# Expert inputs of a mixture layer gathered as 128 half rows instead of 64 whole rows

## What is computed

```
logits = (xf @ w_router) + b_router
top_val, top_idx = lax.top_k(logits, TOP_K)          # 4 of 32
gates = jax.nn.softmax(top_val, axis=-1)
...                                                    # rows sorted by expert
xs = xf[row_tok]
def expert_block(args):
    xb, e = args
    hu = xb @ w_up[e] + b_up[e]
    x_glu = jnp.minimum(hu[:, :D_FF], SWIGLU_LIMIT)
    x_lin = jnp.clip(hu[:, D_FF:], -SWIGLU_LIMIT, SWIGLU_LIMIT)
    act = x_glu * jax.nn.sigmoid(SWIGLU_ALPHA * x_glu) * (x_lin + 1.0)
    return act @ w_down[e] + b_down[e]
out = segment_sum(ys * row_gate, row_tok)             # 2048 rows back to 512 tokens
```

## Time and profile before

| | |
|---|---|
| median of three executions | 2962.32 us |
| the profiled execution, its own time | 2956.22 us |
| its span | 2954.6 us |
| TensorE busy, share of the span | 94% |
| DMA by SP's queue, share of 16 engines | 53.7% (607.76 MB) |
| DMA by POOL's queue | 4.1% (38.12 MB) |
| mean granted TensorE clock | 0.967 |

### The profile page before, as it was taken

The page is one execution under the profiler, slowest core; times in us unless marked ns, Lnnn a source line. Parts: engine busy times, 40 slices in busy tenths (PEclk is TensorE's granted clock), DMA queues, the critical chain, the costliest instruction groups (busy, mean ns, idle before and its releaser), DMA issues.

```text
span 2954.6 us, 37476 instructions
## 1 busy us (share of the span) xinstructions
PE 2770.8 (94%) x15815; PEld 1366.1 (46%) x15815; DVE 1125.3 (38%) x1420; ACT 477.1 (16%) x936; POOL 242.1 (8%) x369
## 2 busy tenths in 40 slices
PE   7998989897889989898999999999999999999998
PEld 3445866332223323232333475467654334556763
DVE  3855454311111111111124253455436652444544
ACT  1113232000000000000001143000023662200001
POOL 1000011112111011110011500000000210000000
PEclk9988988999999999999999999999999999999999
DMA  9776235999999999999999131213132223321310
GB/s 340 286 257 255 74 115 191 385 345 416 384 394 408 409 404 408 407 413 397 413 407 350 9 127 52 86 57 114 57 80 59 66 50 114 107 86 57 114 57 29
DMA packets 172882, 648.23 MB, mean 219 GB/s; under 512 B 75965, under 2 KB 77573, under 8 KB 140305
## 3 DMA queue, kind: packets, MB, share of 16 engines
q1 hardware_dynamic: 156674, 607.76, 53.7%
q0 software_dynamic: 15984, 38.12, 4.1%
q10 hardware_dynamic: 64, 0.07, 0.0%
HBM read 626.43 MB, written 24.06 MB: 220 GB/s over the span
## 4 chain that ended last, share of the span: by engine, by line
PE 78%; DMA 12%; DVE 5%; ACT 2%; DVEq 1%; issue 1%; SPq 0%; ACTq 0%
PE ps L1867 14%; PE ps L2548 10%; PE ps L2583 10%; DMA slots<-in_w_down_dram 8%; PE ps L1905 8%; PE ps L2886 4%; PE ps L2619 4%; PE ps L2257 3%; PE ps L3142 2%; DMA slots<-in_ada_w_dram 2%; PE ps L1913 2%; PE ps L2513 2%; PE ps L2430 2%; PE ps L2533 2%; PE ps L1259 2%; DMA slots<-in_w_ada_dram 2%
## 5 line engine op out<-in xcount | busy, mean ns | idle before, releaser
L1867 PE MATMUL ps<-slots,hT 128*32 128x512 f32 x5120 | 563.2, 598 | 15.4 <-DMA slots<-in_w_up_dram 14.3
L1867 PEld LDWEIGHTS ps<-slots,hT 128*32 128x32 f32 x5120 | 165.5, 111 | 388.3 <-issue 362.6
L2583 PE MATMUL ps<-slots,work 128*128 128x512 f32 x672 | 289.6, 592 | 2.8 <-DVE work L2661 2.8
L1905 PE MATMUL ps<-slots,work 128*32 128x512 f32 x2112 | 247.8, 613 | 45.8 <-DMA slots<-in_w_down_dram 45.3
L2020 DVE TENSOR_SCALAR stage<-ps 128x512 f32<-128x512 f32 (+1 forms) x47 | 32.2, 686 | 549.0 <-PE ps L1871 548.6
L2583 PEld LDWEIGHTS ps<-slots,work 128*128 128x128 f32 x672 | 127.5, 190 | 162.5 <-issue 157.9
L2548 PE MATMUL ps<-hT,slots 128*128 128x256 f32 x768 | 168.7, 379 | 0.0
L1905 PEld LDWEIGHTS ps<-slots,work 128*32 128x32 f32 x2112 | 69.3, 112 | 194.5 <-issue 189.4
L2886 PE MATMUL ps<-hT,slots 128*128 128x512 f32 x352 | 156.8, 601 | 0.0
L2548 PEld LDWEIGHTS ps<-hT,slots 128*128 128x128 f32 x768 | 145.9, 190 | 22.4 <-issue 2.9
L2758 DVE TENSOR_TENSOR work<-work,ps 128x1024 f32<-128x1024 f32 x60 | 71.6, 1218 | 164.8 <-PE ps L2583 164.6
(11 more groups left out here) (610 smaller groups left out, 3447.7 us busy)
## 6 DMA issues: line engine op xcount, KB each, us to landing
slots<-in_w_up_dram SPq DMA_DIRECT2D x128, 2048.0 KB
slots<-in_w_down_dram SPq DMA_DIRECT2D x64, 2048.0 KB
slots<-in_mlp_w_dram SPq DMA_DIRECT2D x32, 2048.0 KB, 7.9
slots<-in_ada_w_dram SPq DMA_DIRECT2D x40, 1024.0 KB, 4.9
slots<-in_w_ada_dram SPq DMA_DIRECT2D x16, 1024.0 KB, 5.4
slots<-in_w_in_dram SPq DMA_DIRECT2D x5, 2048.0 KB
slots<-in_rnn_w_in_dram SPq DMA_DIRECT2D x24, 384.0 KB, 4.2
slots<-in_w_ada_dram SPq DMA_DIRECT2D x4, 2048.0 KB
```

What stands on the lines that cost most here:

```text
L1867: ins = pe.matmul(to, x[:, k, unit * UNIT:(unit + 1) * UNIT], upw[s][:, k % 2, col:col + CH], start=k == 0, stop=False)
L1905: ins = pe.matmul(to, actT[:, 4 * q + j, 64 * u + 32 * h:64 * u + 32 * h + 32], downw[sl[h]][:, j, half * CH:(half + 1) * CH], start=k == ...
L2583: ins = pe.matmul(ps[:, bank + t], x[:, k, t * P:(t + 1) * P], w[:, k], start=k == 0, stop=k == HK - 1)
```

## The change

Each quad is now gathered by 128 indices, 64 rows times two halves: partition `64 h + r` receives half `h` (2 KB) of row `r`. The index table is built with 128 rows, by issuing each of the 16 matmuls of `route_pe` twice, once for output partitions 0 to 63 and once for 64 to 127 with the same operands, and `xsl` holds 2 x token + h. All gathers have 128 indices, those of quads with one unit too; an empty place gets an index beyond the bound as before. A quad then takes four transposes of 128 x 128 in place of eight of 64 rows (or eight for two quads together), one PSUM bank a quad, and ScalarE's copy puts the two halves of the columns in place. The block loop after the passes keeps its gather of 64 whole rows.

```diff
-    k["pairsf"] = ...((pairs + np.array([0, 1]))...
+    rc[:, 241] = r // (2 * UNIT)
+    k["pairsf"] = ...((pairs * np.array([2, 1]) + np.array([0, 1]))...
...
+        h2_halves = h2_dram.rearrange("t (h n) -> (t h) n", h=2)
...
             for a in range(16):
-                ins = pe.matmul(ps[0:64, 4, 0:2 * NQ], in_row[:, a], marks[:, a]..., start=a == 0, stop=a == 15)
+                for h in range(2):
+                    ins = pe.matmul(ps[64 * h:64 * h + 64, 4, 0:2 * NQ], in_row[:, a], marks[:, a]..., start=a == 0, stop=a == 15)
...
-            v.tensor_scalar(xempty, ps[0:64, 4, NQ:2 * NQ], 0.0, float(T), ALU.is_equal, ALU.mult)
+            v.tensor_scalar(xempty, ps[:, 4, NQ:2 * NQ], 0.0, float(2 * T), ALU.is_equal, ALU.mult)
             v.drain()
-            v.tensor_tensor(xsl[:], ps[0:64, 4, 0:NQ], xempty, ALU.add).then_inc(S("route_step"), 1)
+            v.scalar_tensor_tensor(xsl[:], ps[:, 4, 0:NQ], row_half, xempty, ALU.add, ALU.add).then_inc(S("route_step"), 1)
...
-        xg_rest = work[0:64, 6144:7168]
+        xg_rest = work[:, 6144:6144 + CH]
...
+        def x_halves(i, q):
+            return xg[i % 4][:, q * CH:(q + 1) * CH] if q < 2 else xg_rest
...
             for q, units, at in quads(i):
-                n = units * UNIT
-                to = xg[i % 4][q * 64:q * 64 + n] if q < 2 else xg_rest[0:n]
-                g.indirect_dma_start(to, None, h2_dram, bass.IndirectOffsetOnAxis(ap=xsl[0:n, at:at + 1], axis=0),
-                                     bounds_check=T - 1, oob_is_err=False)...
+                g.indirect_dma_start(x_halves(i, q), None, h2_halves, bass.IndirectOffsetOnAxis(ap=xsl[:, at:at + 1], axis=0),
+                                     bounds_check=2 * T - 1, oob_is_err=False)...
...
-                for tile, r0, n, ks in x_runs(i):
-                    for j in range(KT // ks):
-                        if m >= 2:
-                            pe.wait_ge(S("moe_turned_out"), m - 1)
-                        for k in range(ks):
-                            ins = pe.transpose(ps[:, 6 + m % 2, k * n:(k + 1) * n], tile[0:n, (ks * j + k) * P:(ks * j + k + 1) * P], ident[0:n, 0:n])
+                for q, units, at in quads(i):
+                    if m >= 2:
+                        pe.wait_ge(S("moe_turned_out"), m - 1)
+                    for k in range(KT // 2):
+                        ins = pe.transpose(ps[:, 6 + m % 2, k * P:(k + 1) * P], x_halves(i, q)[:, k * P:(k + 1) * P], ident[:])
...
-                        a.copy(xgT[i % 2][:, ks * j:ks * (j + 1), r0:r0 + n],
-                               ps[:, 6 + m % 2, 0:ks * n].rearrange("p (k n) -> p k n", k=ks)).then_inc(S("moe_turned_out"), 1)
+                    a.copy(xgT[i % 2].rearrange("p (h k) n -> p h k n", h=2)[:, :, :, q * n:(q + 1) * n],
+                           ps[:, 6 + m % 2].rearrange("p (k h n) -> p h k n", h=2, n=n)).then_inc(S("moe_turned_out"), 1)
```

More of the change, by code:

```diff
@@ L104, in constants @@
     rc[:, 240] = (r // UNIT) % 2 - 2
+    rc[:, 241] = r // (2 * UNIT)
     k["route"] = rc
-    k["pairsf"] = np.ascontiguousarray((pairs + np.array([0, 1])).astype(np.float32).reshape(P, 16, 2).transpose(0, 2, 1).reshape(P, 32))
+    k["pairsf"] = np.ascontiguousarray((pairs * np.array([2, 1]) + np.array([0, 1])).astype(np.float32).reshape(P, 16, 2).transpose(0, 2, 1).reshape(P, 32))
     return k
@@ L1376, in build @@
         q_edge, w_of, r_base, r_cap = rconst[:, 0:NQ + 1], rconst[:, 64:128], rconst[:, 128:160], rconst[:, 160:192]
-        half_at = rconst[:, 240:241]
+        half_at, row_half = rconst[:, 240:241], rconst[:, 241:242]
         tok_of, dest_of = rconst[:, 256:272], rconst[:, 272:288]
@@ L1390, in build @@
         again = flatT[0:64, 3840:3968]
-        xempty = flatT[0:64, 3968:3968 + NQ]
+        xempty = flatT[:, 3968:3968 + NQ]
         pairs = R0[:, 1800:1800 + 16 * LCOLS].bitcast(I32)
@@ L1394, in build @@
         tab = sb("tab", [1, E + 2 * MAXO + 1], I32)
-        xsl = sb("xsl", [64, NQ], I32)
+        xsl = sb("xsl", [P, NQ], I32)
         ysl = sb("ysl", [P, NQ], I32)
@@ L1454, in route_pe @@
             for a in range(16):
-                ins = pe.matmul(ps[0:64, 4, 0:2 * NQ], in_row[:, a], marks[:, a].rearrange("p two q -> p (two q)"), start=a == 0, stop=a == 15)
+                for h in range(2):
+                    ins = pe.matmul(ps[64 * h:64 * h + 64, 4, 0:2 * NQ], in_row[:, a], marks[:, a].rearrange("p two q -> p (two q)"), start=a == 0, stop=a == 15)
             ins.then_inc(S("route_product"), 1)
@@ L1656, in quads @@
             return [(q, min(UNITS[RANKS[i]] - 2 * q, 2), QBASE[RANKS[i]] + q) for q in range(QUADS[RANKS[i]])]
[L1658 to L1669, removed]
+        def x_halves(i, q):
+            return xg[i % 4][:, q * CH:(q + 1) * CH] if q < 2 else xg_rest
+        x_pieces = [len(quads(i)) for i in range(NPASS)]
         x_piece, act_piece, up_piece = [0], [], []
@@ L1761, in moe_gather @@
             for q, units, at in quads(i):
-                n = units * UNIT
-                to = xg[i % 4][q * 64:q * 64 + n] if q < 2 else xg_rest[0:n]
-                g.indirect_dma_start(to, None, h2_dram, bass.IndirectOffsetOnAxis(ap=xsl[0:n, at:at + 1], axis=0),
-                                     bounds_check=T - 1, oob_is_err=False).then_inc(S(f"xg_in{i % 4}"), 16)
+                g.indirect_dma_start(x_halves(i, q), None, h2_halves, bass.IndirectOffsetOnAxis(ap=xsl[:, at:at + 1], axis=0),
+                                     bounds_check=2 * T - 1, oob_is_err=False).then_inc(S(f"xg_in{i % 4}"), 16)
         def block_list(g, b, n):
@@ L1838, in turn_x @@
                 m = x_piece[i]
-                for tile, r0, n, ks in x_runs(i):
-                    for j in range(KT // ks):
-                        if m >= 2:
-                            pe.wait_ge(S("moe_turned_out"), m - 1)
-                        for k in range(ks):
-                            ins = pe.transpose(ps[:, 6 + m % 2, k * n:(k + 1) * n], tile[0:n, (ks * j + k) * P:(ks * j + k + 1) * P], ident[0:n, 0:n])
-                        ins.then_inc(S("moe_turned"), 1)
-                        m += 1
+                for q, units, at in quads(i):
[3 more added lines that the diff above has]
+                        ins = pe.transpose(ps[:, 6 + m % 2, k * P:(k + 1) * P], x_halves(i, q)[:, k * P:(k + 1) * P], ident[:])
+                    ins.then_inc(S("moe_turned"), 1)
+                    m += 1
             def up(i):
@@ L1985, in x_out @@
                 m = x_piece[i]
-                for tile, r0, n, ks in x_runs(i):
-                    for j in range(KT // ks):
-                        a.wait_ge(S("moe_turned"), m + 1)
-                        a.copy(xgT[i % 2][:, ks * j:ks * (j + 1), r0:r0 + n],
-                               ps[:, 6 + m % 2, 0:ks * n].rearrange("p (k n) -> p k n", k=ks)).then_inc(S("moe_turned_out"), 1)
-                        m += 1
+                for q, units, at in quads(i):
+                    n = 2 * UNIT
+                    a.wait_ge(S("moe_turned"), m + 1)
+                    a.copy(xgT[i % 2].rearrange("p (h k) n -> p h k n", h=2)[:, :, :, q * n:(q + 1) * n],
+                           ps[:, 6 + m % 2].rearrange("p (k h n) -> p h k n", h=2, n=n)).then_inc(S("moe_turned_out"), 1)
+                    m += 1
             x_out(0)
```

## The result

The changed kernel takes 2929.27 us (median of 4 runs, 2923.3 to 2930.05) where the kernel before takes 2961.45 us beside it: ratio 0.9893, 95% interval 0.9878 to 0.9908. A second set of five runs gave 2928.82 us and 0.9891 (0.9875 to 0.9908). That is 32 us less; the forecast was 2930 us, with a range of 2917 to 2960.

What follows compares the result with a forecast made beforehand. Bound: TensorE's chain to about 667 us, then DMA engines to about 1550 us. Terms -31 + 0.5 - 1 - 0.5 = -32 us, 2924 against the profiled 2956.22, so a median of about 2930 us; range 2917 to 2960.

Steps and rivals of the forecast that it cites:

- What bounds it: Claim on the kernel's bound: TensorE's chain up to about 667 us, the DMA engines from then to about 1550 us.
- both regimes: Passes of the mixture: TensorE's chain up to about 667 us, then DMA engines to about 1550 us.
- the waits for weights: Sign of being right: TensorE's waits for weights between 690 us and the end fall by half.
- The gathers: Gathers of x once DMA is the bound: 24 ns lost a row, 37 us for 61/80 of the units, all regained.
- the scatter's end: Loss remaining in the changed gathers: nearly none, like the scatter of y with 128 partitions and 2 KB pieces.
- What comes back: Passes where TensorE has freed no slot for earlier weights: 6 us off the 37, leaving -31 us.
- The index product: Matmuls ahead of the first gather, 16 becoming 32: +0.5 us, between nothing and +2.8.
- The first gather: Issue to landing of the first x, ahead of its transposes: -1 us, between 1.7 earlier and 5.8 later.
- Transposes: Transposes of x on the chain in the first seven passes: -0.2 us a quad, -0.5 us at most.
- Reading is slow: Rival: fetching scattered DRAM rows stalls engines, so 24 ns a row stay; 2961 us, chance 0.14.
- pieces cost: Rival: each gathered piece costs the weight stream a fixed 24 ns whatever its size; about 3005 us, chance 0.07.
- TensorE becomes the bound: Rival: in the passes half or more of the 31 us returns as DMA idling for slots; 2947 us, chance 0.17.

## Why the prediction was right, and where it was not

*What bounds it.* Right in both regimes: 0.5 us gained before the first long DMA piece, 35.4 us after it, and the doubled transposes show that TensorE's time is covered in the second. Of the signs it named, one came out weaker: the waits for weights fell by 40% (63.8 to 38.3 us), not by half.

*The gathers.* I put the loss at 24 ns a row, and took the scatter's end, nothing left. 2 ns a row are left. The 37 us for 61 of 80 units became 35.4 us of shorter chain. The doubt I named, that the scatter runs out of SBUF, was without effect. The reason, however, was only inferred; the runs show what it depends on. Two DMAs of 64 partitions bring the loss back with the same pieces and the same places (20 ns), half rows into the old partitions keep it (24), and consecutive rows keep it (22). The section "Door 1: The DMA port swizzle" of the Trainium skill's page "SBUF — State Buffer", which the prediction named, says that partitions 0 to 63 reach only 8 of the 16 ports, and so agrees with the second and the third; for the first, the rule cited with that run speaks. That ports are the mechanism inside the chip is the page's account; no run here shows a port. The runs show that it takes one DMA over 128 partitions, with the number of its pieces not told apart from its span.

*What comes back.* This was the term mis-sized: 6 us off, where nothing came back that can be told. With 2 ns a row left, the 1562 rows of 61 units in 80 had 37 x 22/24 = 34 us to give, and 35.4 us arrived. DMA idles more at the 6-unit expert (13 us for 7), but all of that stands ahead of the first long DMA piece of the chain, in the regime to which I had given nothing anyway; after it only the 5-unit expert shows more (4 us for 2).

*The index product.* +0.5 us, measured 0: 64 records took 2.82 us where 32 took 2.81.

```profile
524.13 2.82 PE L1458 MATMUL ps<-hT 128*64 128x94 f32 x64 [0.96 <-DVE hT L1557]
...
528.78 1.11 POOL L1757 DMA_INDIRECT work<-h_dram,xsl  x1 [0.95 <-issue]
...
538.36 0.66 PE L1836 MATMUL ps<-ident,work 128*128 128x128 f32 x4 [2.88 <-DMA work<-h_dram,xsl]
```

The two 64-wide tiles run side by side as the 32-wide ones do; the lower bound was the value.

*The first gather.* I took -1 us; from issue to its transposes it is 9.58 us (9.49 in the second profile), where it was 9.37. The median landing went from 10.0 to 9.0 us, not to the scatter's 8.3:

```profile
work<-h_dram,xsl POOLq DMA_INDIRECT x47, 9.0
y_dram<-modB,ysl POOLq DMA_INDIRECT x47, 8.4
```

Gathers land 1 us sooner on the whole, this one didn't; the step failed in reading a median for one instance. The product and this gather were put at -0.5 us together and came to +0.2.

*Transposes.* -0.5 us. The price of a quad was misread: four transposes were taken as half of the 1.04 us of eight, and take 0.66 us, so a quad gains 0.05 us on the 0.71 of before and not 0.2. On the chain before the first long DMA piece five quads have this form, 0.25 of the 0.5 us gained there. The run with twice as many transposes shows that their price is within noise on the whole.

*The rivals.* "Reading is slow" fell to the consecutive rows, "pieces cost" to the half rows in the old partitions, "TensorE becomes the bound" to the doubled transposes; each had its price worked out from rows, and each test was far from it. The sum of 31 + 1 came out near 32 us partly by luck: the passes gave 36, because the 6 us taken off for what comes back were not lost, and the medians differ by 32 because some 4 us went in parts of the program that the forecast doesn't speak of. Two differences of opposite sign, 6 and 4 us, so cancelled in the main.

## What to carry to other kernels

Where DMA engines show a full share but move less than they do elsewhere in the same stage, divide the DMA time lost by the bytes of what runs beside the stream: here a quarter of the rate was lost while gathers landed in 64 partitions or fewer, more than twice their own bytes' time again. Try to let a DMA that runs beside a saturated stream span all 128 partitions in one instruction, even if rows have to be split in halves and the index table doubled; then look for what DMA waits on, which here was the order of the passes.

## What the runs showed of the hardware

A gather of 64 rows of 4 KB into 64 partitions, beside weights that arrive at 427 GB/s, takes away 22 to 24 ns of everybody's DMA time for each 4 KB it moves, on top of the 10 ns that 4 KB need at that rate (22 without an index, 20 as half rows in two DMAs, one to each half of the partitions); in one DMA of 128 half rows over 128 partitions it is 2 ns. I had expected the dependence on partitions. I had not expected it to be set by the single DMA, so that lower and upper halves in two DMAs issued 1.3 us apart lose nearly as much as both in the lower.

Nor had I expected that 188 transposes of 128 x 128 could be added at no cost to a kernel whose TensorE shows 95% busy. About half of them went into waits that the profile shows. The busy time of the whole span rose by 13.4 us (2768.6 to 2782.0) for some 20 us of added work, so a few microseconds of what was shown as busy may have been waiting too; that part is an estimate.
